# Entrance of a two-layer encoder step: another order for the norm weights and the pooling scales, and a first weight tile split in halves

## The reference, cut to what matters

```python
def rms_norm(x, g):
    y = x * lax.rsqrt(mean(x * x, axis=-1) + EPS)
    return y * g
xp = rms_norm(hp, g[0])          # norm_g[layer, 0]
...                              # the rows of xp times ab_w_in[0], 1024 x 1792
mp, cpn = pool_mixer(xp, hist0, pos_p, c_w[li], c_scale[li])   # layer 1; c_scale is first needed here
```

## Time and profile before

| what | us |
|---|---|
| median of 3 runs | 968.04 |
| lowest and highest | 966.71, 968.51 |
| profiled execution, its own time | 966.96 |
| its span, first to last instruction | 965.0 |
| outside the span in it | 1.96 |
| first matmul of block (0, 0) in it | 10.80 after the span's start |

### The profile page before, as it was taken

How to read it: one execution, slowest core, us unless ns; L and a number is a source line. 1 busy time by engine, 2 the same in 40 slices (tenths; PEclk the granted TensorE clock), 3 DMA queues, 4 the chain that set the end, 5 groups by cost and what they waited for, 6 DMA issues and landing times.

```text
span 965.0 us, 17834 instructions
## 1 busy us (share of the span) xinstructions
PE 943.0 (98%) x7032; PEld 908.1 (94%) x7032; DVE 739.9 (77%) x1105; ACT 568.1 (59%) x1081; POOL 48.0 (5%) x57
## 2 busy tenths in 40 slices
PE   7999999999999999999999989999999999999997
PEld 6799889999999999999999978999999999999886
DVE  5487554888799998877679888898999887755643
ACT  5642655887555555556567666876555555654552
POOL 0081220000000000000000001100000000000000
PEclk9999999999999999999999999999999999999999
DMA  8324113466544444457664575454444443656553
GB/s 281 82 70 117 44 46 88 130 190 184 156 140 131 132 135 138 121 143 201 181 178 137 167 189 158 131 154 123 140 131 132 134 141 90 188 169 191 198 171 113
DMA packets 246611, 138.66 MB, mean 144 GB/s; under 512 B 15226, under 2 KB 237794, under 8 KB 246528
## 3 DMA queue, kind: packets, MB, share of 16 engines
q1 hardware_dynamic: 246064, 137.06, 49.2%
q0 software_dynamic: 224, 0.35, 0.2%
q10 hardware_dynamic: 240, 0.10, 0.1%
HBM read 134.91 MB, written 2.58 MB: 142 GB/s over the span
## 4 chain that ended last, share of the span: by engine, by line
PE 88%; DVE 4%; ACT 2%; issue 2%; DMA 2%; POOL 0%; ACTq 0%; DVEq 0%; POOLq 0%
PE ps L815 14%; PE ps L817 13%; PE ps L816 13%; PE ps L1306 12%; PE ps L1310 12%; PE ps L1309 12%; PE ps L1257 3%; PE ps L1259 3%; PE ps L1258 3%; DVE wlo L2099 2%; DMA raw<-in_ffn_w_in_dram 1%; PE ps L1184 1%; ACT whi L1461 1%; DMA scale_rows<-in_c_scale_dram 1%; PE ps L1009 1%
## 5 line engine op out<-in xcount | busy, mean ns | idle before, releaser
L2099 DVE TENSOR_TENSOR wlo<-raw,whi 128x1024 fp32r<-128x1024 f32 (+3 forms) x232 | 230.3, 997 | 82.6 <-ACT whi L1461 82.0
L1461 ACT ACTIVATE whi<-raw 128x1024 fp32r<-128x1024 f32 (+3 forms) x232 | 199.3, 864 | 72.1 <-PE ps L817 54.5
L1306 PE MATMUL ps<-xhi,whi 128*128 128x288 f32 (+1 forms) x528 | 154.2, 292 | 1.0 <-ACT tmp L1995 1.0
L1310 PE MATMUL ps<-xhi,wlo 128*128 128x288 f32 (+1 forms) x528 | 153.6, 291 | 0.0
L1309 PE MATMUL ps<-xlo,whi 128*128 128x288 f32 (+1 forms) x528 | 152.8, 289 | 0.0
L816 PE MATMUL ps<-mlo,whi 128*128 128x288 f32 (+1 forms) x528 | 152.7, 289 | 0.0
L2099 DVE TENSOR_TENSOR wlo<-t,whi 128x1024 fp32r<-128x1024 f32 x86 | 105.1, 1222 | 26.6 <-ACT whi L1461 26.6
L815 PE MATMUL ps<-mhi,whi 128*128 128x288 f32 (+1 forms) x368 | 107.9, 293 | 0.0
L817 PE MATMUL ps<-mhi,wlo 128*128 128x288 f32 (+1 forms) x368 | 107.5, 292 | 0.0
L1306 PE MATMUL ps<-shi,whi 128*128 128x288 f32 x352 | 104.2, 296 | 0.1
L1310 PE MATMUL ps<-shi,wlo 128*128 128x288 f32 x352 | 104.1, 296 | 0.0
(11 more groups left out here) (301 smaller groups left out, 2122.5 us busy)
## 6 DMA issues: line engine op xcount, KB each, us to landing
raw<-in_ffn_w_in_dram SPq DMA_DIRECT2D x177, 256.0 KB, 3.4
raw<-in_ffn_w_in_dram SPq DMA_DIRECT2D x44, 512.0 KB, 4.2
raw<-in_ffn_w_out_dram SPq DMA_DIRECT2D x48, 384.0 KB, 3.7
raw<-in_ffn_w_out_dram SPq DMA_DIRECT2D x48, 320.0 KB, 3.5
raw<-in_ffn_w_out_dram SPq DMA_DIRECT2D x22, 512.0 KB, 4.3
raw<-in_ab_w_in_dram SPq DMA_DIRECT2D x10, 512.0 KB, 5.4
raw<-in_ab_w_out_dram SPq DMA_DIRECT2D x10, 256.0 KB, 3.0
raw<-in_ab_w_out_dram SPq DMA_DIRECT2D x20, 128.0 KB, 3.3
```

The lines of the kernel that those rows point to most:

```text
L1306: mm = pe.matmul(out, wh, hi[:, k, :], start=opens and k == 0, stop=False, skip_group_check=True)
L1310: mm = pe.matmul(out, wl, hi[:, k, :], start=False, stop=k == KC // 2 - 1, skip_group_check=True)
L1461: act.activation(whi[:, m % NSPLIT, 0:n], split_source(m), ACT.Copy).then_inc(w_hi, 1)
L2099: dve.tensor_tensor(wlo[:, s, 0:n], split_source(m), whi[:, s, 0:n].bitcast(F32), ALU.subtract)\
```

## The change

The scales' DMA counts on `tables_loaded`, which now waits for 64 instead of 48; the norm weights need only 16 on `gains_loaded`. TensorE turns the norm weights first, then both halves of tile 0, then makes two filling products; it turns the scales only ahead of block (3, 3). ScalarE takes them out of PSUM after all squares, ahead of the root. Unit 0 is split in two halves of 512 columns (`hi_half`, `lo_half`), each with its own count; the halves alternate with the input's first half, and `lo_no(m)`, one more than `split_no(m)`, replaces it in every wait on `w_lo`. The two matmul triples of block (0, 0) wait for one half each.

```diff
-AB_LOADS, TABLE_LOADS = 16 * 6, 16 * 3
+AB_LOADS, TABLE_LOADS = 16 * 6, 16 * 4
+def lo_no(m):
+    return split_no(m) + 1
# TensorE, va_block
-                pe.wait_ge(w_lo, split_no(m))
                 pe.wait_ge(first_lo, 2 * t + j // 2 + 1)
...
                 for c in range(2):
+                    pe.wait_ge(w_lo, lo_no(m) - (c == 0 and m == 0))
# TensorE, order
-            turn_first(0, (0,))
-            pe.wait_ge(gains_loaded, 32)
+            pe.wait_ge(gains_loaded, 16)
             pe.transpose(flat(7, 0, 64), gain_rows[:, :], ident[0:64, 0:64]).then_inc(gains_turned, 1)
-            turn_first(0, (1,))
-            fill(4, 2)
-            pe.wait_ge(gains_ready, 1)
-            pe.transpose(flat(7, 64, KC), scale_rows[:, :], ident[0:KC, 0:KC]).then_inc(gains_turned, 1)
+            turn_first(0)
+            fill(2, 2)
             for t, j in FIRST_BLOCKS:
+                if (t, j) == (3, 3):
+                    pe.wait_ge(tables_loaded, TABLE_LOADS)
+                    pe.transpose(flat(7, 64, KC), scale_rows[:, :], ident[0:KC, 0:KC]).then_inc(gains_turned, 1)
# ScalarE
-            act.dma_start(scale_rows[:, :], ...).then_inc(gains_loaded, 16)
+            act.dma_start(scale_rows[:, :], ...).then_inc(tables_loaded, 16)
-            hi_part(0)
+            hi_half(0)
             high_first(0, 0)
+            hi_half(1)
             hi_part(1)
             high_first(0, 1)
-            act.wait_ge(gains_turned, 2)
-            act.activation(gains[:, 64:72], flat(7, 64, 8), ACT.Copy).then_inc(gains_ready, 1)
             keep_first_rows(0)
...
             for t in range(2, NT):
                 square_first(t)
+            act.wait_ge(gains_turned, 2)
+            act.activation(gains[:, 64:72], flat(7, 64, 8), ACT.Copy).then_inc(gains_ready, 1)
             root_first()
# VectorE
-                dve.wait_ge(w_hi, split_no(m))
+                dve.wait_ge(w_hi, lo_no(m))
             scale_first(0, 0)
-            lo_part(0)
+            lo_half(0)
             low_first(0, 0)
+            lo_half(1)
             scale_first(0, 1)
...
             invert_first()
+            dve.wait_ge(gains_ready, 2)
```

More of the change, by code:

```diff
@@ L687, in raw_free @@
                         if SPLIT_UNITS[m]:
-                            sp.wait_ge(w_lo, split_no(m))
+                            sp.wait_ge(w_lo, lo_no(m))
                         else:
@@ L888, in _ @@
             m = U_IN + 4
-            pe.wait_ge(w_lo, split_no(m))
+            pe.wait_ge(w_lo, lo_no(m))
             for b in range(2):
@@ L1081, in _ @@
                     for early in range(2):
-                        pe.wait_ge(w_lo, split_no(U_OUT + early))
+                        pe.wait_ge(w_lo, lo_no(U_OUT + early))
                         if early == 0:
@@ L1091, in _ @@
                 else:
-                    pe.wait_ge(w_lo, split_no(U_OUT + u))
+                    pe.wait_ge(w_lo, lo_no(U_OUT + u))
                     if 3 <= e < 8:
@@ L1332, in fast_rest @@
                     early = f == 0
-                    pe.wait_ge(w_lo, split_no(ma))
+                    pe.wait_ge(w_lo, lo_no(ma))
                     if early:
@@ L1347, in fast_rest @@
                         term(ma, 0, 2 + f % 2, *s1, n, True).then_inc(w_used, 1)
-                    pe.wait_ge(w_lo, split_no(mb))
+                    pe.wait_ge(w_lo, lo_no(mb))
                     pe.wait_ge(sum_kept, 2 * i + 1)
@@ L1477, in _ @@
             act.dma_start(gain_rows[0:64, :], norm_g.rearrange("l j (k p) -> (l j k) p", p=P)).then_inc(gains_loaded, 16)
-            act.dma_start(scale_rows[:, :], c_scale[0].rearrange("(k p) -> k p", p=P)).then_inc(gains_loaded, 16)
+            act.dma_start(scale_rows[:, :], c_scale[0].rearrange("(k p) -> k p", p=P)).then_inc(tables_loaded, 16)
             act.wait_ge(pool_set, 1)
@@ L1497, in square_first, with hi_half @@
                                accum_out=ssq[0:n, t:t + 1]).then_inc(x_squared, 1)
+            def hi_half(c):
+                act.wait_ge(w_loaded[LOAD_SEM[0]], loaded(0))
+                act.activation(whi[:, 0, c * AW:(c + 1) * AW], raw_part(0, UNIT)[:, c * AW:(c + 1) * AW], ACT.Copy)\
+                    .then_inc(w_hi, 1)
             act.wait_ge(gains_turned, 1)
             act.activation(gains[:, 0:64], flat(7, 0, 64), ACT.Copy).then_inc(gains_ready, 1)
-            hi_part(0)
+            hi_half(0)
             high_first(0, 0)
+            hi_half(1)
             hi_part(1)
             high_first(0, 1)
-            act.wait_ge(gains_turned, 2)
-            act.activation(gains[:, 64:72], flat(7, 64, 8), ACT.Copy).then_inc(gains_ready, 1)
             keep_first_rows(0)
@@ L1960, in fast_first @@
                         if layer and f == FC - 1:
-                            act.wait_ge(w_lo, split_no(AT["ta", 1, 0]))
+                            act.wait_ge(w_lo, lo_no(AT["ta", 1, 0]))
                         gelu_gate(f - 1)
@@ L2124, in _, with lo_half @@
             dve.wait_ge(gains_ready, 1)
+            def lo_half(c):
+                dve.wait_ge(w_hi, c + 1)
+                cols = slice(c * AW, (c + 1) * AW)
+                dve.tensor_tensor(wlo[:, 0, cols], raw_part(0, UNIT)[:, cols], whi[:, 0, cols].bitcast(F32), ALU.subtract)\
+                    .then_inc(w_lo, 1)
             scale_first(0, 0)
-            lo_part(0)
+            lo_half(0)
             low_first(0, 0)
+            lo_half(1)
             scale_first(0, 1)
@@ L2664, in first_terms @@
                 if f:
-                    dve.wait_ge(w_lo, split_no(AT["tb", layer, f - 1]))
+                    dve.wait_ge(w_lo, lo_no(AT["tb", layer, f - 1]))
                 halves = raw[:, :].rearrange("p (h n) -> p h n", n=HALF)
```

## The result

The changed kernel took 971.15 us (median of 7 runs) against 968.55 of the kernel before (7 runs); the ratio is 1.0025, 95% interval [1.0014, 1.0035], so 1.4 to 3.4 us slower. The prediction was 968.3 with a range to 969.7. Of the gap between forecast and measurement 0.5 us is the base: the kernel before had a median of 968.04 in three runs and 968.55 in seven. The profiled execution has a span of 969.3 against 965.0.

The account below looks back on a forecast made before the run. The prediction took a nearly gapless TensorE matmul stream, hung on the first matmul, as the bound. Start +0.07 and scales +0.17 made 0.24 us more, 968.04 to 968.3, range 966.9 to 969.7.

Parts of the forecast that it names:

- The rest: Remaining edits, among them two fewer fills (0.96 us of TensorE) and a later load of unit 3: worth nothing.
- the peg: First matmul of block (0, 0), on which the matmul stream hangs: from 10.80 to 10.46, 0.34 us earlier.
- the clock: TensorE's clock level at the entrance; whether transposes count for its rise, the trace before could not tell.
- rival B: Slower: clock rises only after block (0, 0), six matmuls take 1.38 us more; 969.3 us, chance 0.17.
- G: Time at which the norm weights' transpose starts on TensorE: 7.22 before, 6.75 forecast.
- A: The forecast itself: first matmul a third of a microsecond earlier, given back at block (1, 0); 968.3 us, chance 0.58.
- the gain of 0.07: VectorE's chain up to tile 1's low part, counted from its first scale, gains only 0.07 us by the halves.
- S: Start of VectorE's first scale: G + 1.47, so 8.22 against 7.88 before.
- C: Faster: norm weights land early, at 5.45, block (1, 0) 1.23 us earlier; 967.0 us, chance 0.12.
- D: Norm weights land with the scales, at 7.22, block (1, 0) 0.54 us late; 968.75 us, chance 0.13.
- the removed wait: At the entrance, norm weights' transpose no longer waits for the scales' DMA: worth 0.47 us.
- The scales' transpose: Turning the scales at block (3, 3), inside the gapless matmul stream, costs 0.17 us.

Follow-up runs that it names:

- the halves alone: The kernel before with unit 0 split in halves and nothing else changed; 968.45 us, ratio 1.0008 [0.9999, 1.0017].
- the one with early fills: The changed kernel with three more filling products ahead of the wait for the norm weights; 969.13 us, ratio 1.0014 [1.0005, 1.0023].
- the semaphore alone: The kernel before with one edit: the scales' DMA has its own semaphore, so norm weights are turned without waiting for it; 967.54 us, ratio 0.9999.
- the first four experiments: Changed kernel with four fills (1.0009), kernel before with two (1.0020), changed kernel with three added early fills (1.0014), changed kernel with half 0 first (1.0025).

## Why the prediction was wrong

**The step that failed** is in "The rest": "Two fewer fills save 0.96 of TensorE, but also ahead of the peg", and the verdict "Nothing". The fills were costed as work, and their work is worth nothing; their activity was not in the sum. It stood apart, under the clock, as rival B with 0.17. The runs put it first: taken out of the kernel before, the two fills cost 0.20%; put back in the changed one, they take the loss from 0.25 or 0.32% to 0.09%. What I held against it, that TensorE "is now busy without a gap from 6.75 to 10.25", did not quite come true (6.95 to 10.03, then idle to 10.57) and was no protection. The gap could be read from the earlier trace rows: the sum took 1.12 for four transposes, which holds a modelled tail, where they are 0.91 from start to start (7.52 to 8.43). By starts, eight transposes and two fills end at G + 3.04 = 9.79 and four fills at 10.71, not 10.25 and 11.2; with four fills the first matmul started at 10.73, at a G of 7.10, and was not held by them.

**A second term was not in the prediction at all:** the 1.1 us at the end of the program. It is in all ten profiles with unit 0 in halves, with early and late clocks alike, so it accounts for some 1.1 of the 2.6 us between the medians, if the unprofiled runs have it as the profiled ones do. The ratio of the halves alone, 0.08% [-0.01, 0.17], is in line with it.

**Rival B was also priced too low.** I had the six matmuls slow and the eight transposes at full clock, with "up to 1.3 more" for these. Both were slow, so block (1, 0) was 1.60 late in one profile and 2.19 in the other, where my price had 1.13. With these transposes slow, B's price went up to 970.6; the measured 971.15 lies beyond that and beyond the stated range.

**The steps on dependencies held.** With G as measured (6.95, I had 6.75) the scale came 1.49 behind it (1.47), the low part of the input 1.39 behind the scale (1.41), the first matmul 2.13 (2.24). At a high clock, with four fills, low(1, 0) started 6.32 behind the scale (6.34) and block (1, 0) 8.56 behind G (8.64). The peg came earlier and VectorE's chain gave it back at block (1, 0), as forecast under A. The reason given for the gain of 0.07 is incomplete, though: a stall of 0.26 gone and an operation 0.05 longer make 0.21; the rest goes because VectorE, free at S + 1.20, waits until S + 1.41 for the input's high part. The norm weights' transpose started at 6.65 to 7.10 in the seven profiles in which their DMA released it, and at 7.09 to 7.35 in the four that waited for the scales too: C fell, and the truth lies between A and D, the removed wait being worth some 0.3 instead of 0.47. Counted from TensorE's first transpose, which starts when the identity has landed, it is 1.55 in the two such profiles whose norm weights' DMA ended the wait, and 1.76 to 1.83 in the four that waited for the scales too.

**The scales' transpose** was mis-sized: 0.38 for 0.17. I scaled it by columns; what it costs is to change over and back. Taking the scales out of PSUM ahead of the root was hidden by the stream, as said: TensorE waits nowhere at unit 4.

**The sum by the runs:** the version with four fills is 0.9 us above the kernel before (0.09% [0.00, 0.18]; I had 0.24), and the late clock makes the rest, 1.5 to 2.2. The 0.9 hold entrance, scales and end together. In the profiles these are 0.72 at the first matmul of unit 4 (43.48 for 42.76, of which 0.38 is the scales' transpose) and 1.1 at the end, 1.9 in all at the span, so profiles and runs agree only within a microsecond.

**What stays open.** Two fills left the whole first block slow in all four profiles that have them alone. In the changed order with four fills, or their length in transposes, the clock rose in the first, the third and the fourth matmul. So activity ahead of the block decides much, and the execution decides a part.

The second place near 570 us goes along with the first. The low level behind the stall lasts 6.8 us in all five profiles whose first block is slow through its third matmul, and in the one with early fills; in the eight others it is 3.4. TensorE resumes there at 567.53 to 570.07 in the six and at 566.34 to 567.70 in the eight. What a late entrance costs in the medians may hold a part from there; why the stretch is then longer was not tested.

Versions whose block (1, 0) is 0.4 to 0.7 earlier in their profiles are not faster in the median. For those with the halves the end explains it; for the semaphore alone, whose span is 0.4 shorter, the effect is below what the runs tell. Within one kernel, time and clock go together: of the 32 runs of the kernel before beside the first four experiments, 21 have a mean granted clock of 0.994 and take 968.5 on average, 10 have 0.995 and take 967.0. The profile before (966.96) has 0.995, so the 4.3 us between the two profiles overstate the loss.

## What to carry to other kernels

Filler products ahead of a dense stream are not idle work to be trimmed: before removing or moving any, look at what TensorE does between its first instruction and the first real matmul, and whether the steps of the first matmuls stay at 0.23 or go to 0.43. A step saved in front of the stream pays only as far as the next engine's chain lets it, here one block. A tiny transpose costs next to nothing ahead of the stream and 0.38 us inside it. And the stretch from the last computing step to the end of the span is a row to compare too: a change at the start of this kernel made it 1.1 us longer.

## What the hardware showed that I had not expected

- The granted clock column reads 1.00 from the span's start in the changed kernel's profiles, while the matmuls of the first block are 0.43 apart. At the entrance only the distance from matmul to matmul tells the level.
- The transposes of this kernel count for the clock. Four in place of two fills gave 0.9997 where two fills alone gave 1.0020, and 1.0007 where the changed kernel gave 1.0032. The Trainium skill (TensorE: Matmul & The Clock Gate, Part 4: PE-mode transpose) says that transposes don't count as busy in the same way. By that rule both would have behaved like the kernels without them, and the measurement decides against it for these float32 transposes; the trace names them MATMUL like the fills and doesn't show in which mode they run.
- With the same instructions ahead of it the level rose at different times, by the steps of the chain: within the transposes from 13.50 to 14.90 us in one profile of the changed kernel, between 15.7 and 16.0 in the other, where the chain still has a step of 0.43 at 15.26.
- The end of the program got 1.1 us longer by a change at its start: from the last VectorE step to the end of the span it is 3.85 to 3.87 us in four profiles and 4.87 to 5.03 in the ten of versions with unit 0 in halves, where a packet of the instruction queue runs within the last 2 us; the cause was not tested.
